# Loading the second expert's up weights as soon as their block is read out, without waiting for the first gather and the last tile's stores

## The reference

```
hn = rmsnorm(h)                              # rows that the experts read
expert, gates = top group, then top 2 experts in it (router on hn)
def expert_block(xb, e):                     # xb: the rows sent to expert e
    h = silu(xb @ w_eg[e]) * (xb @ w_eu[e])  # gate and up: 1024 x 512 each
    return h @ w_ed[e]                       # down: 512 x 1024
out[token] += gate * expert_block row        # both picks of a token
```

## Time and profile before

| what | value |
|---|---|
| median of three runs | 1043.31 us (1042.52 to 1043.85) |
| profiled execution | 1045.51 us |
| its span, first to last instruction | 1043.7 us |
| PE busy | 994.2 us (95%) |
| DVE busy | 563.6 us (54%) |
| HBM traffic over the span | 263 GB/s |
| granted clock of PE, mean | 0.989 |

### The profile page before, as it was taken

How to read it: one execution, slowest core, us unless ns; L and a number is a source line. 1 busy time by engine, 2 the same in 40 slices (tenths; PEclk the granted TensorE clock), 3 DMA queues, 4 the chain that set the end, 5 groups by cost and what they waited for, 6 DMA issues and landing times.

```text
span 1043.7 us, 33213 instructions
## 1 busy us (share of the span) xinstructions
PE 994.2 (95%) x14570; PEld 788.2 (76%) x14570; DVE 563.6 (54%) x1285; ACT 244.1 (23%) x531; POOL 105.4 (10%) x169
## 2 busy tenths in 40 slices
PE   7999999999999999999989999999999999999976
PEld 6795858585868686847788898888788787887832
DVE  1433535353535344427856766766665756556627
ACT  2362323232322322122111111111111011111125
POOL 0110101010101010101111111011011110110000
PEclk8999999999999999999999999999999999999988
DMA  9921010000000000656999999999999999999858
GB/s 319 340 82 41 1 41 0 40 0 40 0 40 0 40 0 40 242 200 248 382 360 414 422 421 424 418 424 420 419 422 417 425 414 420 419 416 423 350 202 361
DMA packets 55329, 263.24 MB, mean 252 GB/s; under 512 B 11384, under 2 KB 12984, under 8 KB 47066
## 3 DMA queue, kind: packets, MB, share of 16 engines
q1 hardware_dynamic: 44506, 235.19, 56.0%
q0 software_dynamic: 8192, 18.06, 4.5%
q10 hardware_dynamic: 2592, 9.44, 2.3%
HBM read 247.18 MB, written 27.19 MB: 263 GB/s over the span
## 4 chain that ended last, share of the span: by engine, by line
PE 74%; DMA 21%; DVE 2%; issue 1%; ACT 1%; SPq 1%; DVEq 0%; ACTq 0%; POOLq 0%
PE bank L1496 19%; DMA arena<-in_w_ed 18%; PE bank L1787 17%; PE bank L1617 11%; PE bank L1799 8%; PE bank L1548 6%; PE bank L1806 4%; PE bank L1477 2%; DMA arena<-pick_rows 1%; DMA arena<-in_w_in 1%; PE bank L1597 1%; PE bank L1555 1%; PE bank L1614 1%; PE bank L1608 1%; PE bank L1878 1%
## 5 line engine op out<-in xcount | busy, mean ns | idle before, releaser
L1496 PE MATMUL bank<-xnT,arena 128*128 128x128 f32 x1728 | 201.5, 278 | 5.1 <-DMA arena<-in_w_in 3.8
L1496 PEld LDWEIGHTS bank<-xnT,arena 128*128 128x128 f32 x1728 | 197.1, 193 | 7.5 <-DMA arena<-in_w_in 4.1
L1787 PEld LDWEIGHTS bank<-hnT,arena 128*64 128x64 f32 x4096 | 156.2, 137 | 9.6 <-issue 4.6
L1787 PE MATMUL bank<-hnT,arena 128*64 128x88 f32 x4096 | 159.3, 239 | 2.6 <-DVE hnT L1287 1.6
L1617 PE MATMUL bank<-arena,mixT 128*128 128x512 f32 x256 | 111.7, 593 | 0.0
L1799 PE MATMUL bank<-arena,osq 128*32 128x384 f32 (+1 forms) x768 | 85.7, 487 | 10.7 <-DMA arena<-in_w_ed 10.7
L1617 PEld LDWEIGHTS bank<-arena,mixT 128*128 128x128 f32 x256 | 47.9, 190 | 57.2 <-issue 57.1
L1309 DVE TENSOR_SCALAR mixT<-mixT 128x352 f32<-128x352 f32 x32 | 13.7, 428 | 136.9 <-ACT mixT L874 136.9
L1278 DVE STREAM_TRANSPOSE hnT<-xs 32x256 f32<-32x256 f32 x192 | 83.6, 435 | 7.3 <-DMA xs<-hn_rows,idx_i 1.2
L1787 PE MATMUL bank<-xnT,arena 128*64 128x88 f32 x2176 | 85.6, 239 | 1.5 <-issue 1.5
L1799 PE MATMUL bank<-arena,silu_r 128*32 128x384 f32 x720 | 80.3, 487 | 6.0 <-DMA arena<-in_w_ed 3.7
(11 more groups left out here) (265 smaller groups left out, 1061.6 us busy)
## 6 DMA issues: line engine op xcount, KB each, us to landing
arena<-in_w_eu SPq DMA_DIRECT2D x32, 2048.0 KB, 25.2
arena<-in_w_ed SPq DMA_DIRECT2D x31, 2048.0 KB, 25.4
arena<-in_w_eg SPq DMA_DIRECT2D x17, 2048.0 KB, 24.6
work<-in_w_eg SPq DMA_DIRECT2D x15, 2048.0 KB, 25.9
hn_rows<-hs ACTq DMA_DIRECT2D x18, 512.0 KB, 3.5
arena<-pick_rows SPq DMA_DIRECT2D x18, 512.0 KB, 11.5
arena<-in_w_in SPq DMA_DIRECT2D x4, 2048.0 KB, 13.0
arena<-in_w_out SPq DMA_DIRECT2D x2, 2048.0 KB, 11.0
```

The lines of the kernel that those rows point to most:

```text
L1496: last = mm(bank[n][:, m * P:(m + 1) * P], w[:, k, m * P:(m + 1) * P], xnT[:, k, :], start=k == 0, stop=k == KD - 1)
L1787: last = mm(out[q * SW:(q + 1) * SW, n * BLOCK:(n + 1) * BLOCK], w[:, k, m * P + q * SW:m * P + (q + 1) * SW], rowsT[b][:, k, :], start=k ...
```

## The change

Two waits on SP go. The load of expert 1's up weights no longer waits for the first gather to land (`rows_in[0]`) nor for the stores of the last tile's rows (`hn_stored`); it waits only for PE's last read of block 5 (`pe_half_out` at 2), as it did before beside these.

```
             load_piece(1, 0, GATE)
             sp.wait_ge(s["pe_half_out"], 1)
             load_piece(1, 0, UP)
-            sp.wait_ge(rows_in[0], 16)
-            sp.wait_ge(s["hn_stored"], 16 * PICKS * TILES)
             sp.wait_ge(s["pe_half_out"], 2)
             load_piece(0, 1, UP)
             sp.wait_ge(s["pool_out_ready"], 2)
```

## The result

The changed kernel is slower: 1051.97 us (four runs, 1050.56 to 1053.28) against 1043.58 us for the kernel before in its four runs, a ratio of 1.0072, 95% interval 1.0061 to 1.0084. That is some 7.5 us by the ratio and 8.4 by the medians. The forecast was 1045.8 us in a range of 1042.9 to 1048.0: the direction is right, the size is three times what was said.

The account below looks back on a forecast made before the run. From 549 us one continuous DMA stream was taken to set the experts' end, so only its start matters. Terms: -0 + 3.0 - 0.5 = +2.5 us, median 1043.31 to 1045.8 us, range 1042.9 to 1048.0.

Parts of the forecast that it names:

- What the removed wait cost: nothing: SP at 478 to 487 us: issuing the load 8.8 us earlier gains 0, since expert 1 needs it only after 505.05.
- The gather has no slack and is held up by the load: First gather, slack at most 0.1 us: lands 3.1 us later behind the load, so expert 0 starts 3.0 us later.
- The wait itself: First gather's data, due at 481.5 us, waits until the load ends at 484.2.
- The mis-sized term: First gather from load's end at 484.2 to landing at 487.1, between examples of 2.45 us (alone) and 3.3 us (pair).
- The clock stays up in the gap: PE idle 483.98 to 487.1 us, 3.1 us: the forecast's sum has no term for a clock fall.
- a rival with a chance of 0.15: PE's clock falls in the gap before expert 0, losing 1.8 us more: +4.3, 1047.6 us, chance 0.15.
- The price of the clock: After the gap before expert 0: no term in the forecast; the clock-fall rival had 4 us at low clock, 1.8 us.
- The shift passes to the end through the load at 526.69, less half a microsecond: Expert stage: 3.0 us shift moves that load to 529.7 and the stream behind it; 0.5 us given back at PE stalls.
- the stall of 1.50 us: PE stall at 530.81 us: keeps its place relative to the load of 526.69, so it stays.
- Expert 1's gather and the stores are hidden: Stores land about 488.5, gather issued 492.5 and landed 497.3, before its rows are turned at 501.5: no added delay.
- The forecast's mechanism alone: Load delays first gather, expert 0 starts 3.0 us later, 0.5 given back: +2.5 us at the end, clock staying up.

Follow-up runs that it names:

- the last two experiments: Kernel before with only the wait for the last tile's stores removed, 1044.17 us; kernel before with the load put behind both gathers, stores' wait gone, 1043.91 us.
- 118 fillers: The changed kernel with 118 filler matmuls instead of 44 on PE ahead of the first gathered rows: 1046.42 us, ratio 1.0028.
- The run without filler: The kernel before, both waits in place, without the 44 filler matmuls ahead of the first gathered rows: 1047.78 us, ratio 1.0033.
- a late gather: The kernel before, both waits in place, first gather issued about 4.3 us later: 1051.77 us with 44 filler matmuls, 1048.22 us with 118.
- the last experiment: The kernel before with expert 1's up-weight load put behind expert 1's gather, both removed waits gone, load issued at 493.08: 1043.91 us, ratio 0.9994.

## Why the prediction was wrong

- *What the removed wait cost: nothing.* Right. The runs with half of the load early, with the load at 483.7 and with the load at 493.1 all take the time of before.
- *The gather has no slack and is held up by the load.* Right, and shown both ways: 8.4 us to landing with the load ahead, 4.1 with it behind. The size was off by a microsecond: 3.1 us were taken, 4.3 came. The wait itself was sized well (2.7 us forecast, 2.5 measured). The mis-sized term is the time from there to the landing. It was put at 2.9 us, between the examples of a gather alone and a pair of gathers; it took 4.3, from 482.5 to 486.81, with the load's last 0.18 MB and then the stores beside it, which have nearly twice the gather's packets (259 to 144). That the stores caused it is argued from these rows; no run isolated it. Against this, not all of the delay reached expert 0: in the traces of the last two experiments PE waits some 0.5 us for the ranks behind the first half of L1757, which a later gather hides. With the clock up (118 fillers) L1757 was 4.3 us late and expert 0 only 3.6.
- *The clock stays up in the gap.* Here the prediction failed. It held the fall for a rival with a chance of 0.15, though the gap it forecast itself, 3.1 us, was longer than the 2.7 us after which the clock was down at the end of the kernel. What was set against that row, the filler matmuls ahead of the gap, had no row behind it: in the changed kernel PE ran them from 479.9 to 482.5, and the clock fell all the same, 4.4 us later. The run without filler shows that even 2.5 us of idle time bring it down in this place.
- *The price of the clock.* The forecast put it at nothing, and the rival had 1.8 us, from a rise after 4 us of work, taken from the start of the kernel. At this place the clock stayed low for 10 us, in the changed kernel and in the one without filler. The price measured is 3.4 us without any delay, 3.2 beside a late gather, 4.6 in the changed kernel. With 10 us in place of 4, the rival's own sum, 10 x (1 - 2.05/3.78), gives 4.6. That is most of the 3.2 us by which the rival's +4.3 stayed short of the measured 7.5.
- *The shift passes to the end through the load at 526.69, less half a microsecond.* Right. Against the last experiment's trace that load is 7.5 us late, the next 7.0, and the end 7.4; with 118 fillers the three are 3.2, 2.8 and 2.7. Against the trace of before the first of them is 9.4 late and the next 7.6, which looks like a give-back at the stall of 1.50 us. It isn't one: the stall is missing too in the last experiment's trace, where the weight queue was as full between 528 and 549 us as before (DMA share 0.99, in the changed kernel 0.81) and the time that of before. What made it in that one execution is not known. The prediction built on it only in saying that it would stay.
- *Expert 1's gather and the stores are hidden.* Right in the changed kernel: the gather issued at 495.81 landed in 4.2 us, and nothing on the chain waits for it.

The forecast's mechanism alone is the run with 118 filler matmuls: 2.9 us, close to the 2.5 that were forecast. In part that is luck, since two errors go against each other: the gather's delay was 4.3 us instead of 3.1, and 0.6 to 0.7 us of it were absorbed at the ranks, which the prediction didn't have. The clock adds 3.2 to 4.6 us. The upper figure is itself the difference of the two kernels' ratios, so that it adds up with 2.9 to the measured 7.5 shows nothing; the independent ones are 3.2 and 3.4, which give 6.1 to 6.3 us, against a measured 6.4 to 8.8, each with an uncertainty of about 1 us.

## What to carry to other kernels

A wait ahead of a large load may be there for what it keeps off the DMA queues: before it is removed, list the small transfers that are issued while the load would run, and ask of each who waits for it and with what slack. When a change opens a gap on PE, treat the fall of the clock as the likely case as soon as the trace holds one fall after a gap of that size, and price it with the work that follows at that place. Fillers sized to a gap of before protect nothing once the gap grows. And read a difference of a microsecond between two traces against a third one: here a stall that only one execution had looked like time given back.

## What the runs showed of the hardware

- Without filler, the clock fell after a gap of only 2.49 us, and did so 1.7 us after PE had resumed work (482.6 to about 484.3). PE had been busy for 1.4 of the 4.6 us up to the end of the gap. With the late gather and 44 fillers it fell 2.6 us into the gap, in the changed kernel 4.4 us into it.
- The way back took 10 us with PE busy all the time (88x88 and 128x88 float32 matmuls, 486.9 to 497 and 484.3 to 494.5), but 4 us at the start of the same kernel (128x128 float32 matmuls).
- A load that was issued first kept transfers on other queues waiting as long as it filled the engines: 2.5 us without a packet for a gather issued 2.1 us behind it, and 9.6 to 11.4 us to landing for stores issued 0.6 us behind it, which take 3.1 to 4.1 in the kernel before. A gather issued 1.7 us ahead of the load was not slowed at all (4.1 us). That is against the turns packet by packet of the Trainium skill (DMA: Bandwidth & Descriptors, Queues, rings and completion order). Who was issued first is not the whole rule either: from 484.0 to 486.8 us the stores moved 246 packets and the gather, issued 2.3 us ahead of them, its last 52.
